# Token shift of the first two tiles moved into the input projection; constants of the prompt mixing moved behind its first chains

## The reference

```
h  = LayerNorm(x)                          # all 1168 rows, width 1024
p  = h @ w_in                              # width 2464
pr, pm = p[:, :1792], p[:, 1792:]
prev   = pr shifted down by one token      # the row before; first row: a given buffer (zero for the prompt)
pr_s   = pr + mu_shift * (prev - pr)       # "token shift"
r, k, v, wd, ad, gd = split(pr_s)          # 512, 512, 512, 64, 64, 128
w = exp(-c * sigmoid(decay_base + tanh(wd) @ w_decay_up));  a = sigmoid(aaa_base + ad @ w_aaa_up)
kk = normalise(k * k_k) per head;  kt = k * (1 + (a - 1) * k_a)
S  = S*w - (S kk)(kk*a)^T + v kt^T         # per head, token by token; y = S r  (RWKV-7)
q, c, kr from pm by RMS norms and rotary;  attention over the compressed latent (MLA), chunk-causal
x <- LN1(alpha*x + [rwkv, mla] @ w_out);  x <- LN2(alpha*x + relu(x @ w_up)^2 @ w_down)
```

## Time and profile before

| | |
|---|---|
| median of 3 runs | 2065.2 us (2061.5 to 2069.67) |
| the profiled execution, its own time | 2070.0 us |
| its span in the profile | 2067.8 us |
| TensorE busy | 1895.7 us (92% of the span) |
| VectorE busy | 934.5 us (45%) |
| ScalarE busy | 670.2 us (32%) |
| GpSimd busy | 356.3 us (17%) |
| mean granted TensorE clock | 0.949 of full speed |

### The profile page before, as it was taken

How to read it: one execution, slowest core, us unless ns; L and a number is a source line. 1 busy time by engine, 2 the same in 40 slices (tenths; PEclk the granted TensorE clock), 3 DMA queues, 4 the chain that set the end, 5 groups by cost and what they waited for, 6 DMA issues and landing times. The chain is left out here.

```text
span 2067.8 us, 39290 instructions
## 1 busy us (share of the span) xinstructions
PE 1895.7 (92%) x16543; PEld 1621.1 (78%) x16543; DVE 934.5 (45%) x1810; ACT 670.2 (32%) x1318; POOL 356.3 (17%) x330
## 2 busy tenths in 40 slices
PE   6999995888898898898877999999999999999997
PEld 6999993666666666666665888999999999899996
DVE  7610105455666655655425365333354333543335
ACT  2221211234344444444323113333343333333332
POOL 0000004322322221221110041300003100032100
PEclk9999996779999999999788999999999999999999
DMA  6452111101210110100133514444434444444441
GB/s 223 139 202 68 65 44 54 47 5 45 77 40 21 58 58 2 57 33 26 52 99 135 193 52 121 129 126 122 126 119 151 138 127 122 123 142 141 127 128 61
DMA packets 167889, 196.28 MB, mean 95 GB/s; under 512 B 18786, under 2 KB 142458, under 8 KB 166580
## 3 DMA queue, kind: packets, MB, share of 16 engines
q1 hardware_dynamic: 165556, 186.35, 28.7%
q0 software_dynamic: 2192, 7.93, 1.0%
HBM read 165.82 MB, written 29.25 MB: 94 GB/s over the span
## 5 line engine op out<-in xcount | busy, mean ns | idle before, releaser
L675 DVE TENSOR_TENSOR c_wo_lo<-c_raw,c_wo_hi 128x1024 fp32r<-128x1024 f32 x94 | 115.2, 1225 | 454.9 <-ACT c_wo_hi L602 454.7
L821 PE MATMUL c_pY<-c_wo_hi,c_hl 128*128 128x512 f32 x564 | 221.3, 392 | 0.0
L821 PE MATMUL c_pY<-c_wo_lo,c_hh 128*128 128x512 f32 x564 | 221.0, 392 | 0.0
L821 PE MATMUL c_pY<-c_wo_hi,c_hh 128*128 128x512 f32 x564 | 220.5, 391 | 0.0
L602 ACT ACTIVATE c_wo_hi<-c_raw 128x1024 fp32r<-128x1024 f32 x94 | 99.7, 1061 | 325.0 <-PE c_pY L821 325.0
L562 POOL TENSOR_TENSOR c_hid<-c_relu 128x384 f32<-128x384 f32 x96 | 79.3, 826 | 669.7 <-ACT c_relu L617 669.7
L853 PE MATMUL c_pU<-c_zT_hi,c_wo_hi 128*128 128x384 f32 x768 | 151.3, 338 | 1.7 <-DVE c_zT_lo L670 1.6
L853 PE MATMUL c_pU<-c_zT_lo,c_wo_hi 128*128 128x384 f32 x768 | 148.6, 334 | 0.0
L853 PE MATMUL c_pU<-c_zT_hi,c_wo_lo 128*128 128x384 f32 x768 | 148.5, 334 | 0.0
L853 PEld LDWEIGHTS c_pU<-c_zT_hi,c_wo_hi 128*128 128x128 f32 x768 | 137.7, 188 | 10.2 <-DVE c_zT_lo L670 2.7
L853 PEld LDWEIGHTS c_pU<-c_zT_hi,c_wo_lo 128*128 128x128 f32 x768 | 134.5, 188 | 0.0
(11 more groups left out here) (463 smaller groups left out, 3444.8 us busy)
## 6 DMA issues: line engine op xcount, KB each, us to landing
c_raw<-w_down SPq DMA_DIRECT2D x96, 512.0 KB, 3.6
c_raw<-w_up SPq DMA_DIRECT2D x96, 512.0 KB, 4.7
scratch_p<-a_o SPq DMA_DIRECT2D x72, 154.0 KB, 1.8
a_w<-w_in SPq DMA_DIRECT2D x8, 1232.0 KB, 8.3
m_prev<-scratch_p SPq DMA_DIRECT2D x8, 896.0 KB, 4.6
m_pr<-scratch_p SPq DMA_DIRECT2D x5, 1232.0 KB, 5.3
b_pr<-scratch_p SPq DMA_DIRECT2D x4, 1232.0 KB, 5.3
scratch_h<-a_x POOLq DMA_DIRECT2D x9, 512.0 KB, 4.5
```

Source lines behind the costliest of these rows:

```text
L675: dve.tensor_tensor(row_lo[slot_of(U)], row_raw[U % 2][:, :], row_hi[slot_of(U)].bitcast(F32), ALU.subtract).then_inc(S("row_lo"), 1)
L821: last = pe.matmul(pY[2 * t + half][:, :], x, w[:, 512 * half:512 * half + 512], start=first and a == 0, stop=final and a == 2, skip_group ...
```

## The change

1. In the last chunk of the projection the tile order is 0, 1, 2, ..., 9 (the meta rows first), in the last but one it stays 1, ..., 9, 0.
2. At the start of the last but one chunk SyncE waits until every store so far has landed, then loads the first 1792 columns of tile 0 and the rows one token earlier; at that chunk's seventh step it does the same for tile 1. In the last chunk, after two steps, it waits for the stores again and loads the remaining 672 columns of both tiles.
3. VectorE computes the token shift of tiles 0 and 1 in the projection, behind the split of the last weights: three operations a tile, in place.
4. The prompt mixing has no `shift_diff` and no `shift` for tiles 0 and 1, no loads of their rows, and no waits for them. `load(0)` and `load(1)` bring the rotary table alone. The dummy products of tile 0's `turn_latent` no longer wait for `sh_mu`.
5. Two orders that the loads used to give are now waits of tile 1: GpSimd's `kk` waits for `KT_src` and `b_ready` of tile 0, ScalarE's `decay` for the transposed `KT` and for `BT_src` of tile 0.
6. The constants move: GpSimd's two memsets to tile 0's `lora_up`, between `kk` and the scaling of `a`; VectorE's ten operations to tile 0's `latent_keys`, between `keys` and the copies into `kTall`. VectorE's memset of ones stays first.
7. Buffers: the projection's row ring and raw weights now lie in `M` (`ring`, `pr0`, `pr`), so that rows can stay where the mixing reads them; the probabilities, their transposes, `khBT`, `mixed` and some buffers of the sample mixing lie in the same memory.

```diff
+EARLY = 2
+        def tiles_of(half, more):
+            return list(range(NW)) if more or half == 0 else [NW - 1] + list(range(NW - 1))
...
-                    for w in range(NW):
-                        store_p((c + half) * NW + w, c + half, (NW * half + w) % 4, w)
+                    for m, w in enumerate(tiles_of(half, more)):
+                        if not more and (half, m) in ((0, 0), (1, EARLY)):
+                            for slot in range(4):
+                                sp.wait_ge(S(f"p_stored{slot}"), 16 * ((c + half) * NW + m) // 4)
+                        if not more and (half, m) == (0, 0):
+                            load_shifted(0)
+                        if not more and (half, m) == (0, 6):
+                            load_shifted(1)
+                        if not more and (half, m) == (1, EARLY):
+                            for i in range(EARLY):
+                                t0, n = TILES[i]
+                                sp.dma_start(rows_early[i][0:n, C_RWKV:C_IN], io["p"][1 + t0:1 + t0 + n, C_RWKV:C_IN])\
+                                  .then_inc(S("rest_landed"), 16)
+                        store_p((c + half) * NW + m, c + half, (NW * half + m) % 4, w)
...
             w_low(N_CH - 1, 1)
+            dve.wait_ge(S("weights_landed"), 16 * len(mix_loads(io, M)))
+            for i in range(EARLY):
+                n = TILES[i][1]
+                p_, past = rows_early[i][0:n, 0:C_RWKV], past_early[i][0:n, 0:C_RWKV]
+                dve.wait_ge(S(f"early_landed{i}"), 32)
+                step(dve.tensor_tensor(past, past, p_, ALU.subtract))
+                step(dve.tensor_tensor(past, past, M["mu"][0:n, :], ALU.mult))
+                step(dve.tensor_tensor(p_, p_, past, ALU.add))
...
-    return steps
+    return [(s, i, v) for s, i, v in steps if i >= EARLY or s not in ("shift_diff", "shift")]
...
                     if i == 0:
-                        pe.wait_ge(S("sh_mu"), 1)
                         spin(pe, SC[:, 0:512], ident, four_const, 3)
...
-            pool.memset(vbd[:, :], 0.0).then_inc(S("vbd_zero"), 1)
-            pool.wait_ge(S("vbd_zero"), 1)
-            pool.memset(kTall[QH:QH + 1, :, :], 0.0).then_inc(S("later_clear"), 1)
-            pool.wait_ge(S("later_clear"), 1)
...
+                if s == "lora_up" and i == 0:
+                    pool.memset(vbd[:, :], 0.0).then_inc(S("vbd_zero"), 1)
+                    pool.wait_ge(S("vbd_zero"), 1)
+                    pool.memset(kTall[QH:QH + 1, :, :], 0.0).then_inc(S("later_clear"), 1)
+                    pool.wait_ge(S("later_clear"), 1)
...
+                if s == "latent_keys" and i == 0:
+                    dve.memset(qT[QH:QH + 1, :, 0:CHUNK], -1e30).then_inc(S("first_set"), 1)
+                    dve.memset(qT[QH:QH + 1, :, CHUNK:P], 0.0).then_inc(S("first_set"), 1)
+                    for m in (CM, QM, PM):
+                        step(dve.memset(m, 0.0))
+                    for m in (IA, X0):
+                        for ck in range(2):
+                            R = rows_of(P, ck)
+                            step(dve.tensor_copy(m[R, :, :], ident[R, R].unsqueeze(1).to_broadcast([CHUNK, HEADS, CHUNK])))
+                    dve.memset(state[:, :, :], 0.0).then_inc(S("state_ready"), 1)
```

More of the change, by code:

```diff
@@ L136, in phase_project @@
         S = Semaphores(nc, io["semaphores"], "a_")
-        x = [sb(f"a_x{i}", [P, D]) for i in range(RING)]
-        g_row, b_row = sb("a_g", [P, D]), sb("a_b", [P, D])
+        x = [M["ring"][:, i, :] for i in range(RING)]
+        g_row, b_row = M["ring"][:, 4, :], M["ring"][:, 5, :]
+        rows_early = [M["pr0"], M["pr"]]
+        past_early = [M["ring"][:, 2 * i:2 * i + 2, :].rearrange("p a d -> p (a d)") for i in range(EARLY)]
         ident = sb("a_ident", [P, P])
@@ L141, in phase_project @@
         hT = [sb("a_hT_hi", [P, KD, TOKENS], F32R), sb("a_hT_lo", [P, KD, TOKENS], F32R)]
-        w_raw = [sb(f"a_w{i}", [P, KD, CH]) for i in range(2)]
+        w_raw = [rows_early[i][:, :].rearrange("p (k n) -> p k n", k=KD) for i in range(2)]
         w_hi = [sb(f"a_wh{i}", [P, KD, CH], F32R) for i in range(2)]
@@ L254, in pair @@
                 for half in range(2):
[L255 to L258, removed]
+                    for m, w in enumerate(tiles_of(half, more)):
+                        u = NW * half + m
+                        drain((c + half) * NW + m, u % 4, w, c * 4 * NW + 16 * (u // 4))
+                        if m == 1 and (half == 0 or more):
                             w_high(c + half + 1, 1 - half)
@@ L363, in project, with pair @@
                 last.then_inc(S("p_filled"), 1)
-            def pair(c):
+            def pair(c, more):
                 for half in range(2):
                     pe.wait_ge(S("w_lo"), c + half + 1)
-                    for w in range(NW):
-                        pe.wait_ge(S("p_drained"), (c + half) * NW + w - 3)
-                        project((NW * half + w) % 4, half, w)
+                    for m, w in enumerate(tiles_of(half, more)):
+                        pe.wait_ge(S("p_drained"), (c + half) * NW + m - 3)
+                        project((NW * half + m) % 4, half, w)
             pe.wait_ge(S("ident_landed"), 16)
@@ L386, in _ @@
             with pe.Fori(1, N_CH // 2 - 1) as j:
-                pair(2 * j)
-            pair(N_CH - 2)
+                pair(2 * j, True)
+            pair(N_CH - 2, False)
 BLK = 3
@@ L1147, in phase_mix_prompt @@
         vall, vmeta, vbd = sb("b_v", [P, SEQ // P, W]), mixed[0:META, 0:W], sb("b_vbd", [P, W])
-        Pb = [sb(f"b_P{i}", [P, SEQ]) for i in range(2)]
-        PTb = [sb(f"b_PT{i}", [P, SEQ // P, P]) for i in range(2)]
+        Pb = [M["ring"][:, i, :] for i in range(2)]
+        PTb = [M["ring"][:, 2 + i, :].rearrange("p (k n) -> p k n", n=P) for i in range(2)]
         OT = sb("b_OT", [P, PAIRS, P])
@@ L1188, in chunk_no, with wait_shifted, wait_rows @@
             return 0 if i == 0 else 2 * i - 1 + c_
+        def wait_shifted(eng, i):
+            if i >= EARLY:
+                eng.wait_ge(S("shifted"), i + 1 - EARLY)
+        def wait_rows(eng, i):
+            if i >= EARLY:
+                eng.wait_ge(S(f"pr_landed{i % 2}"), 16 * (i // 2))
         def key_jobs(i):
@@ L1268, in _ @@
                     pe.wait_ge(S("la_ready"), 2 * i + 2)
[L1269 removed]
+                    wait_shifted(pe, i)
                     turns("loraT", lambda b: [(b[0:LORA, 0:n], la[0:n, :]),
@@ L1761, in _ @@
             dve.memset(laT[LORA:LORA + 1, :, :], 1.0).then_inc(S("ones_set"), 1)
[L1763 to L1771, removed]
             for s, i, v in schedule(vector=True):
```

65 lines of the change are left out of this document (43 added, 22 removed).

## The result

| | median, us | runs | ratio to the kernel before, 95% interval |
|---|---|---|---|
| before | 2064.69 | 8 | |
| changed | 2051.93 (2049.02 to 2066.57) | 8 | 0.9946 [0.9921, 0.997] |
| changed, again with the experiments | 2050.01 (2046.95 to 2066.73) | 8 | 0.9928 [0.9902, 0.9953] |

Predicted were 2047 us (2037 to 2057). The profiled execution has a span of 2051.3 us, 16.5 less than before.

The account below looks back on a forecast made before the run. TensorE's wait for tile 0's multiply at the head of the prompt phase was taken as the bound. The terms -16.3 + 3.0 - 4.5 gave -17.8 us, from the median 2065.2 to 2047, range 2037 to 2057.

Parts of the forecast that it names:

- What bounds the kernel: Prompt phase head: TensorE waits 18.9 us for tile 0's multiply by mu; time won before tile 1 moves everything behind.
- the signs of being wrong: TensorE gap in the last two chunks, tile 0's c after 318, constants over 7 us, or a shift shrinking between tiles.
- Part 1: Head of the prompt phase: tile 0's turn_latent at 317.0 instead of 333.31, a gain of 16.3 us.
- The three legs: Paths to tile 0's turn_latent: squares and norm to 316.9, dummy products to 316.3, rotary key to 316.6.
- The cover of the six operations: Six shift operations, 12 us in all, hide in the projection where VectorE idles for 56 us.
- Price 0 for SyncE's waits: SyncE's three waits and loads in the projection delay stores, not products: price 0, bound 3 us.
- Part 2: Constants behind tile 0's first chains: the long memset holds VectorE, copies into kTall late; loss 3.0 us, bounds 0.2 and 8.
- the table's landing: Rotary table at the phase's start: landed in 3.6 us; 2 us sooner would make the kTall copies 1 to 2 late.
- Part 3: Tile 1 beside tile 0's Newton steps: turn_latent of tile 1 at 368.9 instead of 373.44, a further gain of 4.5 us.
- The clock: TensorE's granted clock may stay high from 366 to 386: at most 4.8 us gain, 0 put into the sum.
- given back: Rival: tile 2's shift, its loads or the attention wait for something unmoving, 17.8 us lost, 2065 us; chance 0.08.
- Slower by the clock of the later tiles: Rival: from 600 to 900 the clock falls in each tile's waits, costing 38 us at 0.85, to 2085; chance 0.07.

Follow-up runs that it names:

- r8: r4 with four more VectorE memsets ahead of its constants, to make VectorE late again; 2055.29 us, ratio 0.992.
- r4: The changed kernel with GpSimd's two memsets moved behind the last operation of tile 0's products; 2043.08 us, ratio 0.989.
- r3: The changed kernel with the early shift for tile 0 alone, tile 1 loaded and shifted in the prompt mixing again; 2052.94 us, ratio 0.9942.
- r5: r4 with the early shift for tile 0 alone; 2051.43 us, ratio 0.9922.
- r0: The changed kernel again, with no edit, timed with the experiments; 2050.01 us, ratio 0.9928.
- r10: r7 without the 16 dummy products in tile 0's grams; 2039.74 us, ratio 0.9873.
- r7: r4 plus dummy products in two TensorE waits, 6 ahead of tile 0's turn_lora and 16 ahead of tile 1's turn_latent; 2042.71 us, ratio 0.9881.
- r9: r4 without the 16 dummy products in tile 0's grams; 2047.00 us, ratio 0.9903.

## Why the prediction was right, and where its sizes were off

**What bounds the kernel**: right. The wait for L1554 is gone, and everything behind moved with it. But it did not move by one amount: the shift shrinks from -18.1 at tile 1 to -12.8 at tile 4, which the prediction lists among the signs of being wrong. Both steps down are the clock's.

**Part 1**, -16.3 forecast: -15.8 at `turn_latent`, -16.0 at `c`. The three legs met as worked out: squares to 313.2, norm with its 1.19 us stall beside `kk` to 317.2, dummies to 317.5. From the phase's start the two are -16.4 and -16.6; the phase began 0.6 us later instead of 0.3, but 0.5 of that stood at 97 us already. The dummies took 5.46 instead of 4.47 us: in both the clock is low when they begin, and it comes back 1 us before their end in the profile of before (0.50 until 330.5, 1.00 from 331) and at their end here (0.50 until 317.5). The cover of the six operations held: TensorE 56.09 of 56.20 us. Price 0 for SyncE's waits: right.

**Part 2**, +3.0 forecast (bounds 0.2 and 8): the mechanism was right, to the instruction. The copies came 1.9 us later than the shifted chain alone would bring them (334.04 against 348.48 - 16.3), and TensorE waited 0.8 and 1.0 us for VectorE: +1.8 directly. The over-estimate is in the table's landing: it took 1.8 us (issue 312.05, `kr` from 313.82) and I had counted 3.6, so the memset ended 1.9 us sooner. The prediction had priced that case at 1 to 2. The Trainium skill (SBUF — State Buffer, "Who interferes with whom") was right in both halves, by this trace: a tensor-with-scalar within SBUF was held by a memset of GpSimd and took 2.41 us, while the operations with two SBUF inputs beside it (`c`, `qn`) took 0.47 and 0.60 us. Left out of the sum: what a delay does to the clock. The same 2 us on VectorE cost 2.5 us at tile 2 in r8 and 6.8 in the changed kernel, both against r4 and from the phase's start.

**Part 3**, -4.5 forecast: -4.2 at `c` of tile 1 (changed against r3), -4.5 from the phase's start, so the term itself was right. And TensorE, working its list in order, kept it for another 34 us, as forecast, through 21 us at 0.51 (windows in r3). Then 3.5 us of it went between 389.5 and 401.3, on the same 160 products at 0.50 instead of 0.89. With the memsets late (r4 against r5) the same edit is worth 6.2 at tile 2.

**The clock**, 0 forecast with at most 4.8 us gain: this is the step that was off, and it had the wrong sign. Before it was 0.64 from 366 to 386, after 0.51 from 355 to 376, and once more low at tile 3. Together they took 5.4 us of the gain at tile 1. The prediction bounded the clock on the side of a gain alone; its one price for a loss was put at 600 to 900, and both losses lie ahead of that. What makes the clock fall at these places is not shown.

**Sum**: -16.0 at tile 0, -15.8 at tile 2 (forecast -17.8), -12.7 from tile 4 on, -12.8 and -14.5 in the medians. The forecast's 2047 was 3 to 5 us low: part 1 fell short by 0.5, part 2 cost 1.2 less than forecast, and the 5.4 us that the clock took are the rest. That the measured time lies well inside the range owes something to the range, which is wide enough for a gain of 8 to 28 us. The rival "given back" came in small by its size and not by its cause: no wait for something that stands still took the 5.4 us. "Slower by the clock of the later tiles" did not occur in the mean (0.97 from 584 to 884, as before), though r0 shows its mechanism once, at 7 us.

## What to carry to other kernels

Work moved into an idle engine of the phase before was worth its wait in full at the place where the wait had stood (16.6 us here). How much of it arrives at the end has to be measured. Before setting constants "behind the first chain", look at which operations stand beside them: here a memset of one partition held a 16x8 operation on the chain for 2.3 us, and its place 20 us later moved tile 2 by 7 us, 2 directly and the rest with the clock. Where TensorE is the bound and its granted clock changes, a microsecond won ahead of it was worth anything from nothing (tile 1's shift, by r3) to three (the late memsets, by r4). So judge such edits by the same work between two marks in both profiles and by the clock there, count the marks from a common start (the phase began anywhere from 311.8 to 314.4 us here), and take medians of many runs.

## What the runs showed that I had not expected

- One program loses 7 us in one execution and not in another, at 530 to 602 us, and what differs is the granted clock (0.65 against 1.00 in the last 14.7 us), with all marks before that equal within 0.1 us.
- The 16 dummy products in the chain cost more than they earned: without them tile 2 comes 6.1 us sooner in r10 than in r7, and 1.7 us sooner in r9 than in r4. The 22 in two waits go with a clock of 1.00 from 346 to 376 us (r7, and r10 up to 376) against 0.78 without them (r9); at tile 2 they are worth 4.0 us from the phase's start (r10 against r9), while the medians, 2039.74 and 2047.00, have intervals that overlap.
- TensorE, busy throughout with products on 16-wide tiles, stayed at the low level from 321 to 335 us (14.0 of 14 us busy at 0.51). With the dummy products of 128x128 just before it the same list ran at 1.00 (r7), and then VectorE was the one that was late.
